# Storing a tile pair's seven blocks of inner activations in one transfer

## The reference, cut to what matters

```python
mod = c_act @ w_ada[l] + b_ada[l]
(sh1, sc1, gt1, sh2, sc2, gt2, sh3, sc3, gt3) = jnp.split(mod, N_MOD, axis=-1)
u = modulate(rmsnorm(h, ffn1_norm[l]), sh1, sc1)
h = h + 0.5 * gt1[:, None, :] * swiglu(u, ffn1_w_in[l], ffn1_w_out[l])
...
def swiglu(x, w_in, w_out):
    g, u = jnp.split(x @ w_in, 2, axis=-1)
    return (jax.nn.silu(g) * u) @ w_out
```

## Time and profile before

| | |
|---|---|
| three runs | 2242.51, 2238.12, 2243.41 us (median 2242.51) |
| the profiled execution | 2238.53 us |
| its span, first to last instruction | 2236.8 us |
| PE busy | 2157.6 us |
| VectorE, GpSimd, ScalarE busy | 1287.0, 1291.8, 817.9 us |
| DMA, mean over the span | 106 GB/s |
| issues of `hid_dram<-hid_raw` | 154 of 256 KB |

### The profile page before, as it was taken

How to read it: one execution, slowest core, us unless ns; L and a number is a source line. 1 busy time by engine, 2 the same in 40 slices (tenths; PEclk the granted TensorE clock), 3 DMA queues, 4 the chain that set the end, 5 groups by cost and what they waited for, 6 DMA issues and landing times.

```text
span 2236.8 us, 28157 instructions
## 1 busy us (share of the span) xinstructions
PE 2157.6 (96%) x10363; PEld 1765.9 (79%) x10363; DVE 1287.0 (58%) x1995; ACT 817.9 (37%) x1520; POOL 1291.8 (58%) x1034
## 2 busy tenths in 40 slices
PE   7989999999999999999999999999999999999998
PEld 6778888887887777778787788888778888887887
DVE  6966667757847237655666202243965444458855
ACT  6422222333445314355545201022522333333444
POOL 4878888869854432312212233336778888769852
PEclk8999999999999999999999999999999999999999
DMA  7155555566334210001101113111053333356333
GB/s 274 46 181 174 174 170 175 161 215 221 95 101 145 76 39 1 13 26 38 29 26 35 45 47 122 47 47 46 21 173 124 104 108 112 99 192 214 95 99 113
DMA packets 224522, 236.28 MB, mean 106 GB/s; under 512 B 9967, under 2 KB 154498, under 8 KB 224130
## 3 DMA queue, kind: packets, MB, share of 16 engines
q1 hardware_dynamic: 224386, 234.49, 33.0%
HBM read 185.69 MB, written 48.76 MB: 105 GB/s over the span
## 4 chain that ended last, share of the span: by engine, by line
PE 72%; DVE 12%; ACT 5%; issue 4%; POOL 4%; DMA 3%; SPq 1%; DVEq 0%; ACTq 0%; POOLq 0%
PE ps L2440 28%; PE ps L2497 15%; PE ps L2401 12%; PE ps L2352 11%; POOL w_lo L1010 2%; DMA ada_half<-in_w_ada 2%; DMA x_raw<-hid_dram 1%; DVE x_op L1913 1%; DVE h L2140 1%; SPq L781 1%; PE ps L2582 1%; PE ps L2692 1%; DVE ada_acc L1710 1%; ACT h L1506 1%; DVE h L1969 1%
## 5 line engine op out<-in xcount | busy, mean ns | idle before, releaser
L2440 PE MATMUL ps<-t,w_hi 128*128 128x512 f32 x1280 | 396.9, 391 | 3.1 <-DVE bufs L1933 1.7
L1010 POOL TENSOR_TENSOR w_lo<-w_raw,w_hi 128x512 fp32r<-128x512 f32 x240 | 349.3, 1465 | 68.1 <-ACT w_hi L1265 67.1
L2497 PE MATMUL ps<-x_op,w_hi 128*128 128x512 f32 x1232 | 381.0, 390 | 6.8 <-DVE x_op L1913 6.8
L977 POOL TENSOR_SCALAR w_hi<-w_raw 128x1024 fp32r<-128x1024 f32 x55 | 58.6, 1065 | 468.0 <-PE ps L2352 292.3
L2440 PEld LDWEIGHTS ps<-t,w_hi 128*128 128x128 f32 x1280 | 239.8, 188 | 55.7 <-POOL w_lo L1010 3.6
L1265 ACT ACTIVATE w_hi<-w_raw 128x512 fp32r<-128x512 f32 x240 | 144.5, 626 | 377.0 <-POOL w_raw L1092 182.2
L2497 PEld LDWEIGHTS ps<-x_op,w_hi 128*128 128x128 f32 x1232 | 230.4, 188 | 58.9 <-POOL w_lo L1010 7.6
L1010 POOL TENSOR_TENSOR w_lo<-q,w_hi 128x512 fp32r<-128x512 f32 x132 | 194.2, 1477 | 114.0 <-ACT w_hi L1265 114.0
L2440 PE MATMUL ps<-t,w_lo 128*128 128x512 f32 x640 | 249.7, 390 | 0.0
L2497 PE MATMUL ps<-x_op,w_lo 128*128 128x512 f32 x616 | 239.8, 389 | 0.0
L1913 DVE TENSOR_TENSOR x_op<-x_raw,x_op 128x512 fp32r<-128x512 f32 x154 | 165.3, 1085 | 100.3 <-ACT x_op L1275 99.5
(11 more groups left out here) (307 smaller groups left out, 4266.9 us busy)
## 6 DMA issues: line engine op xcount, KB each, us to landing
w_raw<-in_ffn_w_in SPq DMA_DIRECT2D x88, 512.0 KB, 4.1
hid_dram<-hid_raw SPq DMA_DIRECT2D x154, 256.0 KB, 4.9
x_raw<-hid_dram SPq DMA_DIRECT2D x154, 256.0 KB, 2.7
ada_half<-in_w_ada SPq DMA_DIRECT2D x112, 256.0 KB, 2.8
w_raw<-in_w_in SPq DMA_DIRECT2D x41, 512.0 KB, 3.9
q<-in_ffn_w_out SPq DMA_DIRECT2D x6, 2816.0 KB, 13.5
ada_full<-in_w_ada SPq DMA_DIRECT2D x16, 512.0 KB, 12.9
x_tile<-in_x SPq DMA_DIRECT2D x8, 512.0 KB, 5.6
```

The costliest lines, as they stand in the source:

```text
L977: nc.gpsimd.tensor_scalar(w_hi[:, slot, :], w_raw[:, slot, :], 1.0, 0.0, ALU.mult, ALU.add).then_inc(w_high, 1)
L1010: nc.gpsimd.tensor_tensor(lo, src, hi.bitcast(F32), ALU.subtract).then_inc(hs_ready, 1)
L2440: mm = nc.tensor.matmul(ps[bank][:], w[i], x[:, k, :], start=(first and k == 0 and q == 0), stop=(k == 3 and q == 2), skip_group_check=True)
L2497: mm = nc.tensor.matmul(ps[down_bank(p) + m][:], w[:, tile(m)], x_op[:, n % 3, x, :], start=(p in (0, 1, 3) and k == 0 and q == 0), stop=( ...
```

## The change

`hidden_out` returns at once for an even tile. For an odd one it waits for the pair's last sum and issues one transfer of all seven blocks, with the DRAM side `(7, PAIRS, P, HALF)` viewed partition first. The counts of `hid_out` are those of one transfer a pair in place of seven. Buffers, loads and all arithmetic are unchanged.

```diff
             def hidden_out(f, t):
 
+                if t % 2 == 0:
+                    return
                 if t < CLASSIC:
-                    sp.wait_ge(prod_ready, 8 * f + (3 if t == 0 else 8))
+                    sp.wait_ge(prod_ready, 8 * f + 8)
                 else:
-                    sp.wait_ge(tile_step, step(f, t, HT4 if t % 2 else HT1))
-                for what in ((H_B10, H_T2, H_T3, H_B11, H_T4) if t % 2 else (H_B00, H_T1)):
-                    sp.dma_start(hid_dram[what, t // 2], hid_raw[:, what, :]).then_inc(hid_out, 16)
+                    sp.wait_ge(tile_step, step(f, t, HT4))
+                sp.dma_start(hid_dram[:, t // 2].rearrange("j p s -> p j s"), hid_raw[:]).then_inc(hid_out, 16)
...
                 n = tile_hs(f, LAST)
                 sp.wait_ge(hs_used, n + 1)
-                sp.wait_ge(hid_out, 16 * (f * DOWN_STEPS + 7 * (PAIRS - 1)))
+                sp.wait_ge(hid_out, 16 * (f * PAIRS + PAIRS - 1))
...
                 hidden_in(f, 9)
-                sp.wait_ge(hid_out, 16 * (f + 1) * DOWN_STEPS)
+                sp.wait_ge(hid_out, 16 * (f + 1) * PAIRS)
...
                 if t % 2 == 0:
-                    dve.wait_ge(hid_out, 16 * (f * DOWN_STEPS + 7 * (t // 2)))
+                    dve.wait_ge(hid_out, 16 * (f * PAIRS + t // 2))
```

## The result

The change makes the kernel slower: 2256.05 us (median of 7 runs, 2252.93 to 2261.99) against 2243.41 us (7 runs, 2238.12 to 2246.99) beside it, ratio 1.0062 [1.005, 1.0075]. The forecast was 2247.1 us with a range up to 2252.0 us. The direction was right, the size was not: about 14 us by the ratio in place of 4.6. The profiled execution after took 2257.83 us (span 2256.1), that before 2238.53 us (2236.8), so the two traces lie 19.3 us apart, somewhat more than the medians.

What follows compares the result with a forecast made beforehand. TensorE's matmuls cover 2157.6 us of the 2236.8 us span. Terms of 1.1 + 0.2 + 1.1 in feed-forward 1 and 1.1 + 1.1 in feed-forward 2, +4.6 us, on the median 2242.51 give 2247.1 us; range 2238.5 to 2252.0.

Steps and rivals of the forecast that it cites:

- Issues: SP's queue: 132 fewer store issues, pieces issued some 3 to 4.6 us sooner, worth bounded by the ring; no gain counted.
- first store: Tiles 0 and 1 of each feed-forward: same seven blocks behind the same weight loads; 0, at best 0.6 us gained.
- issue-bound rival: First tiles, both feed-forwards: pieces late because issues keep SP; PE's waits there go, 9.6 us faster, 2232.9 us; chance 0.10.
- Tile 3's step: First tiles: even stores gone, first piece up to 1.3 us sooner, PE's waits of 1.8 and 1.7 us shrink; counted 0.
- Tile 4's step: Each feed-forward: two extra blocks ahead of the piece VectorE stands for reach PE; +1.1 us each, least 0.7 us.
- Down phase: Last pair's store carries seven blocks, not five, ahead of the down loads; +1.1 us in each feed-forward (0 to 1.4).
- Steady tiles: Every second step has 1.3 us more ahead of its pieces, the others 1.3 less; +0.2 us (0 to 0.3).
- clock rival: First tiles, both feed-forwards: longer low clock; 8.9 us in all with upper ends; sign: below 1.00 for 6 us; chance 0.18.

Runs made afterwards that it cites:

- experiment 1: Kernel before, with two transfers a pair (two blocks with the even tile, five with the odd) in place of seven single stores: 2242.67 us, ratio 1.0002.
- experiment 5: Kernel before, with one transfer of seven blocks only for tile pairs 4 and 5 to 18 and 19 of feed-forward 1: 2252.91 us, ratio 1.0041.
- experiment 7: Kernel before, with only the last pair of each feed-forward stored in one transfer of seven blocks: 2244.54 us, ratio 1.0014.
- experiment 2: Kernel before, with nothing merged but all seven single stores of a pair issued with the odd tile: 2256.54 us, ratio 1.0064.
- experiment 4: Changed kernel, with PE's column sums moved behind the fourth product of their tile: 2251.74 us, ratio 1.004 to the kernel before.
- 6: Kernel before, with the change applied in feed-forward 2 alone: 2244.11 us, ratio 1.0007.
- experiment 8: Kernel before, with the first two pieces of each step issued ahead of the stores: 2235.36 us, ratio 0.9968.
- experiment 3: Changed kernel, with the first two pieces of each step issued ahead of the store: 2237.51 us, ratio 0.9979 to the kernel before.
- experiment 11: Kernel before, with two transfers a pair, two pieces ahead of the store and column sums behind the fourth product: 2229.82 us, ratio 0.9947.

## Why the prediction was wrong

**Right.** The first reading holds in full: bytes in a full ring decide, not issues. The piece behind tile 3's store was issued at 149.89, as foretold near 150, and landed at 159.09 (foretold near 159), 9.20 us later:

```profile
149.89 9.20 DMA ada_half<-in_w_ada
```

- *Issues* and *first store*, 0: experiment 1 shows it, 1.0002. The issue-bound rival is out.
- *Tile 3's step*, covered: PE's wait for ScalarE stayed (1.9 for 1.8), that for L1933, now L1934, went from 1.7 to 1.3. Less shrank than was foretold, at no cost.
- *Tile 4's step*, +1.1: the column sums of tile 5 start 1.2 us later (165.48 against 164.27), 1.0 of it behind the first product; PE's wait ahead of them grew from 2.4 to 3.8 us. That looks like the term but doesn't show it, for the kernels of experiments 5 and 7, which store these pairs as before, have the same (first product to sums 71.5 and 71.4 us, and these waits):

```profile
PE ps L2402 <- DVE ada_acc L1741: 3.5, 1, 3.5
...
PE ps L2402 <- DVE ada_acc L1741: 3.6, 1, 3.6
```

  In feed-forward 2 the tile loop took 1.5 us more, with 3.3 us of waits in place of 2.1. There the term is borne out: 386.4 to 386.9 us in the four traces with the stores and the order of before (before, experiments 1, 5, 7), 387.4 to 388.6 in the four with the pieces behind a late store (the change, experiments 2, 4, 6).
- *Down phase*, +1.1 each: the down phases grew by 0.9 and 1.5 us, and experiment 7 measures the term by itself. PE's waits in them grew by only 0.8 and 0.3 us (about a microsecond was foretold); in the second a low clock took the rest, which the prediction didn't have. ScalarE gets the x block that it waits for at 544.29, 26.4 us after the store's issue, against 528.26 and 25.5 us:

```profile
544.29 0.63 ACT L1276 ACTIVATE x_op<-x_raw 128x512 fp32r<-128x512 f32 x1 [6.25 <-DMA x_raw<-hid_dram]
```

These places differ by 5.1 us between the two traces, where 4.4 were forecast; in part that is luck, since the first tiles of feed-forward 1 and the stretch behind its down phase differ as much between kernels that leave them alone.

**Wrong: the step *Steady tiles*, "+0.2 us (0 to 0.3)".** From the sums of tile 5 on the trace lost 13.9 us, of which 2.6 (4.26 - 1.63) stand at the low clock behind tile 5 and 11.3 in the steady tiles; by itself the step cost 9.2 us (experiment 5). Two things failed in it.

First, it let the even steps' gain (1.3 us less ahead of their pieces) stand against the odd steps' loss, and looked for cover in one place, PE's gate at the sums of tile 17, as if each step began anew. But the step is a turn of a loop, and an early piece of an even step brings nothing there (VectorE then waits for PE: 20.2 us at L1934 from 170 to 478, where L1933 had 13.5), while a late piece of an odd one moves the next weight load and so the next store. A sign of it could have been read from the trace before: weight loads 39.56 us apart on the mean for two tiles, PE's own need 39.3 us, so the loop was already falling behind. With pieces first (experiment 8) they come 39.09 us apart. The loop was taken for covered because PE showed no idle time. In truth VectorE stood up to 4.9 us for those pieces before the change already, and the longest such wait is 8.9 us now.

Second, it priced a wait at its own length. In these traces the pauses ahead of the sums of tiles 11 and 17, 5.4 us, brought 5.8 us at the low clock behind them (4.19 + 1.65).

**The clock rival** saw this mechanism, but only at tile 5, where its sign is there: rows below 1.00 stand until some 9 us behind the start of the sums, over the 6 us that were to decide, and the stretch behind it took 4.3 us more than the undisturbed 58.97, against 1.6 before. But waits of 3.5 and 3.6 us there, in experiments 5 and 7, brought no more than the 1.6 us, so it isn't shown that the longer pause made the longer low clock. In the first tiles of feed-forward 2 the rival is refuted: the granted clock stayed 1.00 through waits of 3.3 us in five pieces. Its price, 8.9 us in all, was too small because it gave the clock no second and third place in the tile loop.

What is shown: postponement is the cause, within the intervals (2, 3); 9.2 of the 14 us are made in the steady tiles of feed-forward 1 (5); it needs pieces behind the store (3, 6). That it is a loop and not one gate rests on experiment 4 and on the chain. What is argued from the traces only: how the 14 us divide between standing and clock, and at which tiles. Nothing was run that keeps the pauses and holds the clock.

## What to carry to other kernels

Fewer and larger transfers brought nothing here (1.0002 in experiment 1), where single blocks already filled the ring and their landings overlapped. In a queue that is full anyway ask what stands behind the bytes, and put what an engine is waiting for ahead of what nobody waits for soon. Before a term is called covered, measure the mean period of every loop through the queue over many turns (here from weight load to weight load) against that of the engine that bounds, since an engine without idle time doesn't show how near the next loop is. And a pause of TensorE is to be priced with the low clock that may stand behind it, which in the trace of the change cost as much again.

The best kernel found is that of experiment 11: two transfers a pair, two pieces ahead of the store, column sums behind the fourth product; 2229.82 us, ratio 0.9947 [0.9933, 0.9961] to the kernel before and some 26 us below the change.

## What was not expected of the hardware

- The length of a pause doesn't say alone whether the clock falls. Ahead of column sums it fell after every idle time of 2.1 us and more in these traces (the longest 6.1 us, in experiment 5), but also after 1.1 us (the change, tile 17) and 0.6 us (experiment 3, tile 5), and not after 1.7 us (experiment 1, tile 5), where 1.7 us in experiment 8 brought it down. In the down phases it fell behind waits of 2.0 us (feed-forward 2 of experiment 5) and 2.4 us (feed-forward 2 of the change), and not behind one of 3.0 us (feed-forward 2 of experiment 2).
- A transfer of 1.75 MB behaves as seven of 256 KB in a row: the store issued at 148.63 landed at 158.46, behind a weight load that landed at 154.09, which is 4.4 us for 1.835 MB, some 420 GB/s. The first piece issued behind such a store held SP's queue for 1.7 us (at 149.89), 1.1 us (234.73) and 2.5 us (274.26), so that the time saved on issues was in part spent there.
